# The prologue of a decoder layer rebuilt: x loaded in four column pieces, setup work placed between the query products, and the order of keys, scan tables and key pages changed

## The reference: what is computed

```python
z = x @ w_in                       # x: 264 x 2048, w_in: 2048 x 8192
q, k, v, u, gate_a, gate_s = split(z)   # 1024, 1024, 1024, 1024, 2048, 2048 columns
# differential attention, 8 heads x 2 maps of 64: prompt on itself, and each of the 8 new
# positions on 2048 cached keys and values (16 pages of 128, given by a page table)
s = q @ k.T / 8 + rel_bias[bucket(q_pos - k_pos)]      # T5 buckets: distance >= 128 is one bucket
attn = rms_norm((softmax(s[0]) - lam * softmax(s[1])) @ v) * (1 - lam_init)
# S5 branch: 64 groups of 64 complex states, h[t] = abar * h[t-1] + B u[t], y = C h + d u
ssm = g * sigmoid(g @ w_glu),  g = gelu(y)
h = layer_norm(alpha * x + (gate_a * (attn @ w_pa) + gate_s * (ssm @ w_ps)) @ w_out)
y = layer_norm(alpha * h + conv_ffn(h))                # d_ff 5504, causal conv of width 3
```

## Time and profile before

| | us |
|---|---|
| median of 3 runs | 1740.39 (1736.45 to 1743.41) |
| the profiled execution | 1737.55 |
| its span in the trace | 1735.6 |
| prologue, to the end of v0 and the scores behind it | 205.25 |
| TensorE busy | 1660.1 (96%) |
| TensorE waiting, largest single wait | 16.2 |

### The profile page before, as it was taken

The page is one execution under the profiler, slowest core; times in us unless marked ns, Lnnn a source line. Parts: engine busy times, 40 slices in busy tenths (PEclk is TensorE's granted clock), DMA queues, the critical chain, the costliest instruction groups (busy, mean ns, idle before and its releaser), DMA issues. The chain is left out here.

```text
span 1735.6 us, 31618 instructions
## 1 busy us (share of the span) xinstructions
PE 1660.1 (96%) x11736; PEld 1473.4 (85%) x11736; DVE 1121.9 (65%) x1740; ACT 651.6 (38%) x986; POOL 391.2 (23%) x341
## 2 busy tenths in 40 slices
PE   7996999999999999989997999999999999999997
PEld 5884876666677667789997999999999999999996
DVE  1345487878878764567667767777777776555555
ACT  2021134434334322333335544444444444333333
POOL 1044576766866860000001000000000000000001
PEclk9898999999999999999998999999999999999998
DMA  9775899999999996776664557667667675766651
GB/s 224 169 228 169 274 325 368 361 376 384 362 379 378 367 344 213 225 195 177 183 182 121 158 160 209 176 174 195 163 184 188 169 190 143 211 175 181 178 163 51
DMA packets 502962, 393.63 MB, mean 227 GB/s; under 512 B 25439, under 2 KB 451316, under 8 KB 502548
## 3 DMA queue, kind: packets, MB, share of 16 engines
q1 hardware_dynamic: 419908, 325.07, 62.2%
q10 hardware_dynamic: 82944, 67.11, 12.3%
HBM read 385.47 MB, written 7.02 MB: 226 GB/s over the span
## 5 line engine op out<-in xcount | busy, mean ns | idle before, releaser
L708 PE MATMUL bank<-work,weight_ring 128*128 128x264 f32 x2176 | 522.5, 396 | 0.5 <-ACT work L1152 0.5
L1431 ACT ACTIVATE weights_hi<-weight_ring 128x2048 fp32r<-128x2048 f32 (+1 forms) x166 | 309.7, 1866 | 514.6 <-PE bank L1031 386.8
L708 PEld LDWEIGHTS bank<-work,weight_ring 128*128 128x128 f32 x2176 | 412.5, 194 | 94.8 <-issue 25.1
L1899 DVE TENSOR_TENSOR weights_lo<-weight_ring,weights_hi 128x2048 fp32r<-128x2048 f32 (+1 forms) x166 | 369.1, 2224 | 112.6 <-ACT weights_hi L1431 67.5
L627 POOL TENSOR_TENSOR work<-work 128x512 f32<-128x512 f32 x256 | 318.7, 1277 | 95.6 <-DMA work<-in_cache_k 73.9
L1030 PE MATMUL bank<-h_hi,weights_hi 128*128 128x264 f32 x1344 | 331.0, 284 | 0.0
L1031 PE MATMUL bank<-h_lo,weights_hi 128*128 128x264 f32 x1344 | 330.2, 284 | 0.0
L1030 PEld LDWEIGHTS bank<-h_hi,weights_hi 128*128 128x128 f32 x1344 | 253.2, 188 | 0.0
L1031 PEld LDWEIGHTS bank<-h_lo,weights_hi 128*128 128x128 f32 x1344 | 252.7, 188 | 0.0
L657 POOL TENSOR_TENSOR work<-work,ffn_scratch 128x1056 f32<-128x1056 f32 x4 | 9.5, 2407 | 1058.4 <-ACT ffn_scratch L1152 1058.4
L1735 DVE TENSOR_REDUCE work<-work 128x8 f32<-128x512 f32 x256 | 164.5, 677 | 47.8 <-POOL work L627 47.5
(11 more groups left out here) (269 smaller groups left out, 1911.9 us busy)
## 6 DMA issues: line engine op xcount, KB each, us to landing
weight_ring<-in_w_up SPq DMA_DIRECT2D x86, 1024.0 KB, 5.7
work<-in_cache_k SPq DMA_DIRECT2D x256, 256.0 KB, 5.9
work<-in_cache_v SPq DMA_DIRECT2D x128, 512.0 KB, 6.1
weight_ring<-in_w_in ACTq DMA_DIRECT2D x60, 1024.0 KB, 11.5
weight_ring<-in_w_down SPq DMA_DIRECT2D x32, 1024.0 KB, 6.0
weight_ring<-in_w_out SPq DMA_DIRECT2D x16, 1024.0 KB, 6.0
weight_ring<-in_w_down SPq DMA_DIRECT2D x16, 704.0 KB, 4.9
weight_ring<-in_w_proj_attn SPq DMA_DIRECT2D x16, 512.0 KB, 4.2
```

What stands on the lines that cost most here:

```text
L708: last = pe.matmul(bank[(n + m) % 2][:, 0:N], chunk_weight(g, k - c * per, m), tiles[k], start=(k == 0), stop=(k == len(tiles) - 1))
L1431: act.activation(w_hi[:, (j % 2) * KT * P:(j % 2) * KT * P + k_tiles * P].bitcast(F32R), slot3(j, 0, k_tiles).rearrange("p k m -> p (k m)" ...
L1899: dve.tensor_tensor(w_lo[:, cols].bitcast(F32R), slot3(off % SLOTS, 0, k_tiles).rearrange("p k m -> p (k m)"), w_hi[:, cols], ALU.subtract ...
```

## The change

The whole change lies in the prologue.

- **x in pieces.** x of the prompt is loaded in four pieces of 512 columns (512 KB each), each with its own semaphore `x_piece[j]`. Weight chunk 0 is issued between the second and the third piece, chunk 1 behind the fourth, and chunk 3 right behind chunk 2.
- **Eleven products of ones** (`WARM`) stand ahead of the first transpose on TensorE, into bank 7, whose content nobody reads.
- **Transposes of x** go to banks 2, 3, 6 and 7; VectorE copies the even tiles, ScalarE the odd ones. Tiles 0 to 7 come first, then q0 and q1 begin; tiles 8 to 11 stand behind the first 4 products, 12 to 15 behind 8. On VectorE and ScalarE the 16 copies stand ahead of the scan parameters.
- **Shared far bias.** Pages 0 to 14 lie in one bucket, so two one-hot products are made in place of 16, and ScalarE broadcasts the first over 15 pages.
- **Hooks.** Bias products, transposes of start states, C, scan parameters and B, the query rows and the scores of the new positions become hooks inside groups of z products. The query rows stand behind the first quarter of u0.
- **Order.** u1 moves behind k7. On GpSimd `fractions(2)` and `fractions(3)` stand ahead of pages 1 and 3. ScalarE and VectorE follow: `rotation(2)` ahead of the copy of k1, pages 0 and 1 summed ahead of `states(0, 2)`.

```diff
-OH_TOEP, OH_PAGE, OH_NEW = 0, 384, 384 + PAGES * P
+OH_TOEP, OH_PAGE, OH_NEW = 0, 384, 384 + 2 * P
...
-GROUPS = in_pairs("q", 0, H) + [(("u", 0),)] + in_pairs("k", 0, 4) + [(("u", 1),)] + in_pairs("k", 4, H) + [(("v", 0),)]
+GROUPS = in_pairs("q", 0, H) + [(("u", 0),)] + in_pairs("k", 0, H) + [(("u", 1),), (("v", 0),)]
...
+WARM = 11
...
-            sp.dma_start(x_rows[:, 0:2, :], a["x_prompt"][0].rearrange("(c p) d -> p c d", p=P)).then_inc(xs_in, 16)
+            def load_x(j):
+                cols = slice(j * 4 * P, (j + 1) * 4 * P)
+                sp.dma_start(x_rows[:, 0:2, cols], a["x_prompt"][0].rearrange("(c p) d -> p c d", p=P)[:, :, cols]
+                             ).then_inc(x_piece[j], 16)
+
+            load_x(0)
             sp.dma_start(x_rows[0:B, 2, :], a["x_sample"].rearrange("b o d -> (b o) d")).then_inc(xs_in, 16)
+            load_x(1)
+            load_weights(sp, 0)
+            load_x(2)
+            load_x(3)
+            load_weights(sp, 1)
...
             load_weights(sp, 2)
+            load_weights(sp, 3)
...
             for p in range(PAGES):
-                if p == 4:
+                if p == 1:
                     fractions(2)
-                if p == 8:
+                if p == 3:
                     fractions(3)
                 products(0, p)
...
+            for _ in range(WARM):
+                pe.matmul(bank[7][:, 0:P], ones[:, :], ones[:, :], start=True, stop=True)
+
+            def x_columns(j):
+                pe.wait_ge(x_piece[j], 16)
+                if j == 0:
+                    pe.wait_ge(xs_in, 16)
+                for k in range(4 * j, 4 * j + 4):
+                    at = bank[(2, 3, 6, 7)[k % 4]]
+                    wait(pe, (x_dve, x_act)[k % 2], k // 2 - 1)
+                    for c in range(2):
+                        transpose(at[:, c * P:(c + 1) * P], x_rows[:, c, k * P:(k + 1) * P])
+                    transpose(at[:, T:N], x_rows[0:B, 2, k * P:(k + 1) * P]).then_inc(tr, 1)
...
+            x_columns(0)
+            x_columns(1)
+            x_copied(8)
+            z_group((("q", 0), ("q", 1)), {1: lambda: x_columns(2), 2: lambda: x_columns(3), 4: lambda: x_copied(KT)})
...
-                for p in range(PAGES):
+                for p in range(2):
...
+            z_group((("q", 2), ("q", 3)), {3: bias_rows})
...
+            z_group((("q", 4), ("q", 5)),
+                    {1: first_states, 2: lambda: c_columns(0), 3: lambda: c_columns(1), 4: lambda: c_columns(2),
+                     5: lambda: c_columns(3), 6: scan_rows})
...
+            z_group((("q", 6), ("q", 7)),
+                    {4: lambda: b_columns(0), 5: lambda: b_columns(1), 6: lambda: b_columns(2), 7: lambda: b_columns(3)})
...
+            z_group((("u", 0),), {1: query_rows})
...
             z_tile(("k", 2), ("k", 3))
-            z_tile(("u", 1))
             cx(0, 2)
             cx(0, 3)
             z_tile(("k", 4), ("k", 5))
             z_tile(("k", 6), ("k", 7))
+            z_tile(("u", 1))
...
+            z_group((("v", 0),), {2: new_scores})
...
             states(0, 0)
             states(0, 1)
-            reduce_page(0, 0)
-            states(0, 2, lambda: reduce_page(0, 1))
-            reduce_pages(0, 2, 3)
-            states(0, 3, lambda: reduce_page(0, 4))
-            reduce_pages(0, 5, 6)
+            reduce_pages(0, 0, 1)
+            states(0, 2, lambda: reduce_page(0, 2))
+            reduce_pages(0, 3, 4)
+            states(0, 3, lambda: reduce_page(0, 5))
+            reduce_pages(0, 6, 7)
             y_out(0)
-            reduce_pages(0, 7, 8, 9, 10, 11)
+            reduce_pages(0, 8, 9, 10, 11, 12, 13, 14, 15)
```

More of the change, by code:

```diff
@@ L742, in _ @@
-            last.then_inc(tr, 1)
-            for b in range(B):
-                last = pe.matmul(bank[6][:, b * H:(b + 1) * H], table[:, OH_NEW + b * P:OH_NEW + (b + 1) * P],
-                                 rel, start=True, stop=True)
-            last.then_inc(tr, 1)
-            z_tile(("q", 2), ("q", 3))
-            pe.wait_ge(tr_used, KT + 3)
-            pe.wait_ge(x0_in, 64)
-            for k in range(4):
-                last = transpose(bank[4][:, k * P:(k + 1) * P], x0_rows[:, k * P:(k + 1) * P])
@@ L755, in _, with first_states, c_columns @@
+            z_group((("q", 2), ("q", 3)), {3: bias_rows})
+            def first_states():
+                pe.wait_ge(tr_used, 3)
+                pe.wait_ge(x0_in, 64)
+                for k in range(4):
+                    last = transpose(bank[4][:, k * P:(k + 1) * P], x0_rows[:, k * P:(k + 1) * P])
+                last.then_inc(s5_tr, 1)
+                pe.wait_ge(c_in, 64)
+            def c_columns(k):
                 wait(pe, s5_used, k - 2)
@@ L1156, in row @@
                 return s5_rows[0:PAIRS, k * P:(k + 1) * P]
+            for k in range(1, KT, 2):
+                act.wait_ge(tr, k + 1)
+                copy(xtile(k), bank[(2, 3, 6, 7)[k % 4]][:, 0:N]).then_inc(x_act, 1)
             act.wait_ge(rows_in, 48)
@@ L1281, in _ @@
             act.wait_ge(tr, KT + 2)
-            copy(bias_pg.rearrange("p (x j) -> p x j", j=2),
-                 bank[5][:, 0:PAGES * H].unsqueeze(2).to_broadcast([P, PAGES * H, 2])).then_inc(tr_used, 1)
+            for first, end in ((0, PAGES - 1), (PAGES - 1, PAGES)):
+                far = bank[5][:, (first > 0) * H:(first > 0) * H + H]
+                last = copy(bias_pg[:, first * 16:end * 16].rearrange("p (g h j) -> p g h j", h=H, j=2),
+                            far.unsqueeze(1).unsqueeze(3).to_broadcast([P, end - first, H, 2]))
```

134 lines of the change are left out of this document (66 added, 68 removed).

## The result

The changed kernel takes 1715.12 us at the median of 4 runs (1705.69 to 1718.81), the kernel before 1738.42 in the same comparison (1733.49 to 1743.41): a ratio of 0.9855, interval 0.9832 to 0.9878. The gain is 23 us at the medians, where 29 were forecast. The profiled execution took 1714.25 us.

The account below looks back on a forecast made before the run. TensorE, busy for 1660.1 of 1735.6 us, was taken as the bound. Gains of 4.6 + 6.3 + 18.0 = 28.9 us, passed on whole, took the profiled 1737.55 to 1708.6, or 1711 at the median; range 1702 to 1727.

Parts of the forecast that it names:

- the forecast case: Whole kernel: all three prologue gains reach the end, a gain of 21 to 38 us; chance 0.67.
- the start, to the end of q0 and q1: Start of TensorE's work: q0 and q1 done at 37 us, not 41.6; gain 4.6 us (0.9 to 11.7).
- shared bias: Bias products after q0 and q1: 4 + 16 records, 4.8 us in place of 11.1; gain 6.3 us (3.8 to 7.3).
- the wait behind the scan: `cx` behind the fourth scan: wait falls from 16.25 to 0.8 us, 2.6 of clock saved; gain 18.0 us (9 to 18.8).
- the loop: After the prologue: same order and full buffers at its beginning, so the gain of 28.9 us passes through whole.
- low-clock case: At the start: the lower clock adds up to 6.5 us, and q0 and q1 are done at 40.7 at worst.
- Data is not late: At the start: x pieces and chunk 0 there at about 12 us, chunk 1 at 16, wanted after 20.
- The size of the transfers: Loading x: the skill wants 1 MiB per DMA, so 512 KB pieces might come later; the forecast sum stays the same.
- My own signs: Trace checks for start, bias, `cx` wait, prologue end and remaining time; value-page waits growing over 5 us would refute the whole.
- The rival "slower": Query tiles: transposes between products keep TensorE at 1.2 GHz, 7.2 us more per tile; 21 slower, 1761 us; chance 0.04.

Follow-up runs that it names:

- after_again: The changed kernel with no edit, run again for a second trace; 1716.1 us, 0.9869 of the kernel before.
- small_store_again: Second run, with more rounds, of the changed kernel with the Toeplitz row stored reversed and once; 1706.2 us, 0.9821 of the kernel before.
- late_fractions: The changed kernel with GpSimd's fractions(2) and fractions(3) moved back ahead of pages 4 and 8; 1724.6 us, 0.9924 of the kernel before.
- after_light: The changed kernel with value-page loads after the first four cut to 64 of 1024 columns; 1689.7 us, 0.9716 of the kernel before.
- small_store: The changed kernel with the Toeplitz row stored reversed and once (12 KB), not as 128 copies (1.5 MB); 1704.0 us, 0.9812 of the kernel before.
- x_in_one_piece: The changed kernel with x in one 2 MB transfer and all 16 tiles transposed ahead of q0 and q1; 1719.0 us, 0.9890 of the kernel before.
- pad_before_loop: The changed kernel with 130 more products of ones between the keys' transposes and the loop; 1742.9 us, 1.0030 of the kernel before.
- bias_alone: The kernel before with the shared far bias alone, two page products in place of 16; 1732.8 us, 0.9973 of the kernel before.
- light pair: The kernel before and the changed one, both with value-page loads after the first four cut to 64 of 1024 columns; 1718.0 and 1689.7 us.

## Why the prediction was right, and where it was not

**The time:** 1711 was forecast, 1715 measured, inside the range of 1702 to 1727, and the mechanism of the forecast case is the one seen. But the terms were off by up to 8 us, and they cancel: that the sum came out 4 us from the median is in part luck. The clock's share is in each:

| term | predicted gain | measured, profiled pair |
|---|---|---|
| the start, to the end of q0 and q1 | 4.6 (0.9 to 11.7) | 41.6 - 30.3 = 11.3 |
| shared bias | 6.3 (3.8 to 7.3) | 11.1 - 3.1 = 8.0 |
| the wait behind the scan | 18.0 (9 to 18.8) | 18.9 - 3.0 - 1.6 = 14.3 |
| a wait for a weight chunk | none | -1.9 - 1.8 of clock = -3.7 |
| the rest of the prologue, not taken apart | 0 | 0.5 |
| the prologue | 28.9 | 30.4 |
| the loop | 0 | -7.8 |
| what follows | 0 | 0.5 |

- *The start.* The step that failed is the choice of 37 us "nearer to the worst, because the trace shows 14 us of these transposes with the clock still low". That row showed only that transposes do not bring the clock up; it said nothing of whether they let it fall. Behind the products of ones it stayed up. And the low-clock case was priced too high: without those products, in `no_warm`, q0 and q1 were done at 34.4 us, not at my worst of 40.7, since the level rose behind the first four products and not behind all eight. So of the 6.7 us by which I missed, 4.1 are the products of ones and 2.6 this. The reading of the first 30 us as run at 1.2 GHz was right: `no_warm` has the same doubling beside the changed kernel.
- *The bias.* Sized 1.7 us too high for this pair, which puts the gain of 8.0 above the term's own range: the 0.6 us of gaps are not there, the records last 0.12 us and no longer, and the clock did not fall behind them. Whether it falls is not settled by the order. In nine traces of the new order it stayed up in four (the changed kernel, `after_again`, `small_store_again`, `late_fractions`) and fell in five, which cost 1.7 us (`after_light`, `small_store`, `x_in_one_piece`) or 3.3 (`pad_before_loop`, `no_warm`); in `bias_alone` it cost 1.6. With such a fall the term is 4.7 to 6.4 us, about the 6.3 that I took. What decides it stays open.
- *The wait behind the scan.* The order of steps was right, the supplier of the first step was not. I let key products start 4 us behind the first `bu`, from the old distance to the query rows. They started 12.7 us behind it, 92.77 to 105.47: SyncE's queue had first to see the Toeplitz round trip land, about 5 us, and the query rows' own store took 4.5 us longer than before. With that out of the way, in `small_store`, the wait is 0.4 us, which is what I had counted (0.8). But `after_again` has 0.4 too, with the first key product as late (105.30): it lost 2.8 us more to the chunk, so TensorE came to `cx` 3 us later. The two waits trade against each other, and their sum is the better measure, 4.9 and 5.1 us.
- *The chunk.* "Data is not late" was argued for the first 16 us only; the chunks that ScalarE issues during the Toeplitz store I did not count, though that store runs 35 us in the trace of before too. This was the largest thing missed: by `small_store` it and the late query rows cost 9 to 12 us between the medians. It is also the best account of why the medians gained 23 us and not 29: in the four traces of the unchanged new prologue it ended at 174.9, 173.7, 183.5 and 181.3 us, in three of the old one (one of them with the small store) at 202.1 to 205.3, so the profiled pair, with 30.4, is near the favourable end. That the other executions spread in the same way is argued; only one of each kernel was traced.
- *The loop.* That the gain passes through whole holds for the traces of the light pair (21.4 us of prologue, 23.3 of span). The 7.8 us of the first pair are mostly spread: the loop takes 491.7 to 503.8 us in the eight traces with the new prologue and full data, 493.3 to 496.0 in three with the old one. The means are 498.0 and 494.8; whether the 3 us between them are real stays open. The loop's length does not follow that of the prologue: the shortest, 491.7, stands behind a prologue of 183.3 us, the longest behind one of 174.9.
- *The size of the transfers.* Smaller ones did not bring the first data later: the first transpose comes at 6.34 us with pieces (`no_warm`) and at 9.78 with one transfer, and no later wait for a piece stands in any list. What bandwidth a single piece gets is not shown by this.
- *My own signs.* Right by them: q0 and q1 done by 37 us (30.3), the bias under 6 us (3.1, clock 1.00), the first instruction behind v0 at about 176 (174.87). Wrong by them, in the first trace: `cx` waits 3.0 us and not under 2, the rest takes 1537.5 us and not 1530, and the waits for value pages grew by 5.8 us, 13.9 to 19.7, where more than 5 was to mean that the prediction as a whole is wrong. In `after_again` they are 15.2 and `cx` waits 0.4, with the same ratio within the intervals, so that sign was set inside the spread of single traces and could not decide.

The rival "slower" had nothing for it: in q4 and q5, with four transposes after every four products (49.55 to 58.43), the four products take 1.78 us, 0.445 each, which is the upper level.

## What to carry to other kernels

When an order is tightened, list every transfer that now falls into a stretch where the queues are slow, and not only those that the change moves: the store of 128 copies had been harmless for as long as nobody asked for data beside it, and then it cost about 9 of the 33 us that the order was worth. Where three engines and a queue hold each other up in a ring, move the one step that needs least (here two GpSimd instructions) ahead of the bulk. Products of ones before the first data paid here, in the trace, when the data came without a gap behind them; a gap of 2.6 us undid them. One trace to a kernel is not enough where the same instructions give prologues 10 us apart: trace the changed kernel twice before explaining a few microseconds.

## What the runs showed of the hardware

- The granted clock in the stretches reads 1.00 from the first microsecond on, though without the products of ones the first transposes last half as long again and the first products twice as long (0.82 and 0.91 us against 0.52 and 0.46). In this case it can be trusted only from the first change of level on; before that, go by durations.
- Transposes at the start neither brought the clock up (14 us of them) nor, when it was up, let it fall (8.4 us of them among 8 products). Behind a wait of 2.6 us that followed the products of ones, the clock fell 1.3 us into the next transposes, which then ran at the lower level (0.8 us to a tile).
- The same ten small bias products, at the same place between products of z, were followed by a fall of the clock in five traces and by none in four; the 24 products behind them took 12.5 to 13.8 us or 10.8.
- One store of 1.5 MB from eight partitions into DRAM took 35 to 37 us. A 1 MB weight chunk issued beside it landed after up to 31.7 us (`pad_before_loop`), against 12.8 at most in the same stretch of `small_store`. While it ran, from 70 to 76 us of the changed kernel, the DMA engines were busy for 0.50 and moved 64 GB/s, and an issue of ScalarE took up to 14 us. With the store of 12 KB and a read with overlapping rows, which do the same work, the read was issued 4.5 to 6.2 us behind the store. Whether the size of the store or its eight partitions made it slow was not tested.
